# First prompt tile and sample tile taken through the stages side by side, in an encoder-trunk kernel on eight cores

## The reference

```python
h = _rmsnorm(x, norm_g); proj = h @ w_in                      # 1024 -> 4608
a, g_a, u, v, g_b, r_a, r_b = split(proj)
pa  = (trailing-window mean of a, windows 2/4/8/16 per group) - a
y_a = (silu(g_a) * (pa @ w_pool * pool_scale)) @ w_a
y_b = (silu(g_b) * u * (W_s layernorm(v) + b)) @ w_b          # chunks of 128 (64 for samples)
x + (sigmoid(r_a) * y_a + sigmoid(r_b) * y_b) @ w_o, then a final rmsnorm
```

## Time and profile before

| | |
|---|---|
| time, median of 3 runs | 867.98 us (865.93 to 882.57) |
| time of the profiled execution | 866.63 us, slowest core's span 865.2 us, others from 858.9 us |
| TensorE busy | 806.2 us, 93% of the span |
| DVE, ACT, POOL busy | 484.1, 279.5, 143.8 us |
| mean granted TensorE clock, slowest core | 0.972 |
| TensorE in 40 slices of 21.6 us, tenths | `4397998899999999999969999999999999999996` |
| granted clock in the same slices | `9778999999999999999979999999999999999999` |
| the chain that ended last | PE 86%, DMA 6%, POOL 2%, DVE 2% |

### The profile page before, as it was taken

How to read it: one execution, slowest core, us unless ns; L and a number is a source line. 1 busy time by engine, 2 the same in 40 slices (tenths; PEclk the granted TensorE clock), 3 DMA queues, 4 the chain that set the end, 5 groups by cost and what they waited for, 6 DMA issues and landing times.

```text
span 865.2 us, 13033 instructions; the slowest of 8 cores (858.9 to 865.2 us)
## 1 busy us (share of the span) xinstructions
PE 806.2 (93%) x3909; PEld 386.4 (45%) x3979; DVE 484.1 (56%) x739; ACT 279.5 (32%) x463; POOL 143.8 (17%) x353
## 2 busy tenths in 40 slices
PE   4397998899999999999969999999999999999996
PEld 2143443344444444444448644444444444444442
DVE  2334544666557655754457575557564665567445
ACT  3232233324233323332325333324232424242322
POOL 2351003111031102200142220022011201031001
PEclk9778999999999999999979999999999999999999
DMA  8599705551314040305051240315013411320202
GB/s 183 98 143 164 175 1 133 111 195 26 122 61 136 12 135 25 125 5 134 21 208 34 74 147 1 101 46 195 1 41 107 148 48 30 117 90 8 100 1 98
DMA packets 52483, 77.84 MB, mean 90 GB/s; under 512 B 34872, under 2 KB 35012, under 8 KB 52160
## 3 DMA queue, kind: packets, MB, share of 16 engines
q1 hardware_dynamic: 47568, 62.83, 22.2%
q0 software_dynamic: 4848, 14.19, 10.1%
HBM read 64.43 MB, written 18.50 MB: 96 GB/s over the span
## 4 chain that ended last, share of the span: by engine, by line
PE 86%; DMA 6%; POOL 2%; DVE 2%; issue 2%; ACT 1%; SPq 1%; POOLq 0%; DVEq 0%; ACTq 0%
PE ps L330 70%; PE ps L498 14%; DMA xr<-xh 3%; DMA Wo<-w_o 2%; PE ps L455 1%; DVE tmp L413 1%; DMA hT<-xn 1%; PE ps L273 1%; SPq L239 1%; DVE xn L297 0%; POOL Win L239 0%; POOL tmp L368 0%; POOL tmp L366 0%; ACT junk L289 0%; DVE pa L420 0%
## 5 line engine op out<-in xcount | busy, mean ns | idle before, releaser
L330 PE MATMUL ps<-hT,Win 128*128 128x512 bf16 (+1 forms) x2258 | 491.3, 369 | 2.6 <-issue 0.2
L330 PEld LDWEIGHTS ps<-hT,Win 128*128 128x128 bf16 x2304 | 225.7, 99 | 240.2 <-issue 2.4
L485 DVE TENSOR_TENSOR tmp<-ps,tmp 128x512 f32<-128x512 f32 (+1 forms) x72 | 47.6, 662 | 145.4 <-PE ps L330 141.9
L280 POOL TENSOR_SCALAR stats<-stats 128x1 f32<-128x1 f32 (+1 forms) x103 | 20.5, 199 | 616.3 <-ACT junk L289 291.4
L498 PE MATMUL ps<-Wo,mg 128*128 128x512 bf16 x531 | 119.2, 383 | 2.8 <-DMA Wo<-w_o 2.1
L479 ACT ACTIVATE tmp<-ps 128x512 f32<-128x512 f32 (+1 forms) x72 | 41.3, 574 | 141.0 <-PE ps L330 140.9
L498 PEld LDWEIGHTS ps<-Wo,mg 128*128 128x128 bf16 x544 | 53.5, 99 | 67.7 <-issue 4.8
L413 DVE TENSOR_TENSOR tmp<-tmp 128x512 f32<-128x512 f32 (+7 forms) x90 | 60.2, 669 | 37.2 <-ACT tmp L399 24.4
L510 DVE TENSOR_TENSOR xr<-ps,xr 128x512 f32<-128x512 f32 x68 | 46.9, 689 | 50.9 <-PE ps L498 50.8
L330 PE MATMUL ps<-s_bf,Wb 128*128 128x512 bf16 (+1 forms) x284 | 69.8, 367 | 0.2
L330 PE MATMUL ps<-fa,Wa 128*128 128x512 bf16 (+1 forms) x281 | 69.5, 367 | 0.4
(11 more groups left out here) (85 smaller groups left out, 482.8 us busy)
## 6 DMA issues: line engine op xcount, KB each, us to landing
xr<-xp SPq DMA_DIRECT2D x64, 512.0 KB, 6.8
yp<-xr SPq DMA_DIRECT2D x32, 512.0 KB, 2.6
Win<-w_in POOLq DMA_DIRECT2D x18, 512.0 KB, 16.4
Wo<-w_o POOLq DMA_DIRECT2D x2, 1024.0 KB, 17.7
xr<-xs SPq DMA_DIRECT2D x4, 512.0 KB, 4.6
Wa<-w_a POOLq DMA_DIRECT2D x4, 256.0 KB, 20.3
Wb<-w_b POOLq DMA_DIRECT2D x4, 256.0 KB, 21.3
ys<-xr SPq DMA_DIRECT2D x2, 512.0 KB, 4.4
```

The lines of the kernel that those rows point to most:

```text
L330: ins = e.matmul(out=bank[:, 0:cols_n], lhsT=l, rhs=r, start=(i == 0), stop=(i == n - 1))
L485: S.add("dve", lambda e: e.tensor_tensor(out=sa[:, 0:T], in0=ya[:, 0:T], in1=sa[:, 0:T], op=ALU.mult), [kya, ksa], [ksa])
```

## The change

The sample tile becomes the second tile. Tile 0 and the sample tile are prepared together (six subs, all transposed by TensorE), and then pass A, B, M and O side by side; only from the third tile on does each tile go alone. So that both fit, the sample tile's hT, `fa` and `s_bf` share one hT buffer, its normalised v goes to `junk` and its merged rows to `n_buf`. The small copies between `sl` and `carry` or `tails` move from POOL to DVE (the one into `sl` now after the ACT copy, the one back at the group's end). Only two blocks of w_in are loaded ahead of the preparation; the other loads stand between the POOL operations of the six subs, and the last 18 behind them in one row. b_s and final_g are spread at the start, copied by DVE. The halo's products are split per group (`carry_in`). The mixing matrices are loaded by SP.

```diff
-    tiles.insert(min(SAMPLE_AT, NT - 1), Tile(True, 0, False, False))
+    tiles.insert(1, Tile(True, 0, False, False))
...
+            if t.sample:
+                assert b == 1
+                t.hT = v_(hTf[1][:, 0:8 * TS], 8)
+                t.fa = v_(hTf[1][:, 8 * TS:12 * TS], 4)
+                t.s = v_(hTf[1][:, 12 * TS:16 * TS], 4)
+                t.n = v_(junk[:, :], 2)
+                t.mg = v_(n_buf[:, :], 8)
+                t.khT = [("hT", 1, s) for s in range(t.ns)]
+                t.kfa = [("fas", g) for g in range(4)]
+                t.ks = [("ss", g) for g in range(4)]
+                t.kn = ["junk"] * 2
+                t.kmg = [("n", j // 2) for j in range(8)]
...
-        def a_group(t, b, g):
+        def a_group(t, g):
             sl, ksl = next_tmp()
             L = 80 if t.sample else H + TP
+            bank, bk = win_group(t, C_A + g * P)
             if t.sample:
-                S.add("pool", lambda e: e.tensor_copy(out=tv(sl, 0, H, True), in_=tails[:, g, :].rearrange(
-                    "p (s h) -> p s h", s=4)), [("tails", g)], [ksl])
-            else:
-                S.add("pool", lambda e: e.tensor_copy(out=sl[:, 0:H], in_=carry[:, g, :]), [("carry", g)],
-                      [ksl])
-            bank, bk = win_group(t, b, C_A + g * P)
-            if t.sample:
+                tg = tails[:, g, :].rearrange("p (s h) -> p s h", s=4)
                 S.add("act", lambda e: e.activation(out=tv(sl, H, L, True), in_=bank[:, 0:TS].rearrange(
                     "p (s l) -> p s l", s=4), func=AF.Copy), [bk], [ksl])
-                S.add("pool", lambda e: e.tensor_copy(out=tails[:, g, :].rearrange("p (s h) -> p s h", s=4),
-                                                      in_=tv(sl, L - H, L, True)), [ksl], [("tails", g)])
+                S.add("dve", lambda e: e.tensor_copy(out=tv(sl, 0, H, True), in_=tg), [("tails", g)], [ksl])
             else:
-                S.add("act", lambda e: e.activation(out=sl[:, H:L], in_=bank[:, :], func=AF.Copy),
-                      [bk], [ksl])
-                S.add("pool", lambda e: e.tensor_copy(out=carry[:, g, :], in_=sl[:, TP:TP + H]),
-                      [ksl], [("carry", g)])
-            bank2, bk2 = win_group(t, b, C_GA + g * P)
+                S.add("act", lambda e: e.activation(out=sl[:, H:L], in_=bank[:, :], func=AF.Copy), [bk], [ksl])
+                S.add("dve", lambda e: e.tensor_copy(out=sl[:, 0:H], in_=carry[:, g, :]), [("carry", g)], [ksl])
+            bank2, bk2 = win_group(t, C_GA + g * P)
...
+            if t.sample:
+                S.add("dve", lambda e: e.tensor_copy(out=tg, in_=tv(sl, L - H, L, True)), [ksl], [("tails", g)])
+            else:
+                S.add("dve", lambda e: e.tensor_copy(out=carry[:, g, :], in_=sl[:, TP:TP + H]), [ksl],
+                      [("carry", g)])
...
-            S.add("dve", lambda e: e.memset(Wnat_s, 0.0), [], kWns)
-            dma("pool", Wnat_p, ws_v, [], kWnp, "w")
-            dma("pool", Wnat_s[0:64, :, 0:64], ws_v[0:64, :, 0:64], kWns, ["Wns0"], "w")
-            dma("pool", Wnat_s[64:128, :, 64:128], ws_v[0:64, :, 0:64], kWns, ["Wns1"], "w")
+            dma("sp", Wnat_p, ws_v, [], kWnp, "c")
+            dma("sp", Wnat_s[0:64, :, 0:64], ws_v[0:64, :, 0:64], kWns, ["Wns0"], "c")
+            dma("sp", Wnat_s[64:128, :, 64:128], ws_v[0:64, :, 0:64], kWns, ["Wns1"], "c")
```

272 lines of the change are left out of this document (126 added, 146 removed).

## The result

The changed kernel takes 897.51 us (median of 4 runs, 896.86 to 897.86); the kernel before, beside it on the same chip, 868.45. The ratio is 1.034 with a 95% interval of 1.032 to 1.037: slower by more than the scatter, and 15.5 us above the forecast of 882. The profiled execution has 897.6 us, a span of 895.5 on its slowest core (core 7) and 889.5 to 895.5 over the cores.

What follows compares the result with a forecast made beforehand. TensorE, busy 93% of the span, was taken as the bound, its gaps and slow stretches open to change. Start 82.3, stage A 37.3 and the rest 760.9 gave 880.5 us span, plus 1.4: 882 us, range 867 to 893.

Steps and rivals of the forecast that it cites:

- The removed waits: Tile 1 and sample tile: waits for hT, w_o and `pa` with their slow stretches go, 21.5 us off.
- The three products end between 15 and 18 us; I take 16.4.: Start, sub 0: products spreading b_s and final_g precede its scaling; square of sub 1 at 20.8 us.
- the early end: Start: the three products end at 15 us if their rows pass sub 1 by three; sum 1.5 us lower.
- No weight or row load binds here.: Preparation up to stage A: loads cost nothing, with one or two w_in blocks issued per 11.7 us round.
- TensorE waits some 7.6 us: Stage A of the pair: TensorE waits for DVE's 27.3 us of work and resumes at 33.1 us.
- Stage B starts 4.25 later as before.: End of the pair's stage A: stage B starts 4.25 us after TensorE resumes, 37.3 after stage A's start.
- Stage B to the end: From stage B's start to the kernel's end: 789.3 - 21.5 - 10.8 + 3.9 = 760.9 us.
- The small copies: Stage A of later tiles: copies on DVE cost 0.4 us per tile, 2.8 over seven, bounds 0 and 1.25 per tile.
- in full: Rival, stage A of later tiles: nothing absorbs the small copies, 8.8 us instead of 2.8, 888 us; chance 0.20.
- The warm start: Rival, preparation: TensorE stays at 2.4 GHz, 12 us less, 870 us (866 to 875); chance 0.15.
- The reordering does nothing: Rival, whole kernel: gains and losses equal, 868 us, needing a start 14 us shorter than worked out; chance 0.05.
- The short start: Rival, preparation: ACT's round does not close, subs follow their loads, stage A near 50 us, kernel 850; chance 0.08.

Runs made afterwards that it cites:

- e1: Changed kernel with the square and scaling of sub i+1 issued ahead of sub i's transposes, sub i-2's normalization behind them; median span 868.0 us against 893.
- e8: Changed kernel with SP issuing the rows b_s and final_g ahead of sub 1's 512 KB; median span 888.8 us against 893.
- e3: Changed kernel with the loads of cp, w_s and the sample's ln_g and ln_b issued in the rounds of subs 2 and 3; median span 885.6 us against 893.
- e13: e11 with GpSimd's four sample row operations waiting for the sample's last s, at stage B's end; 842.4 us, 0.971 of the kernel before.
- e11: e6 with the sample's n rows in xn buffers, its row operations issued behind stage A, and the w_s buffer's memset ahead of it; median span 842.7 us.
- e15: Changed kernel with the halo's copy into the slab ahead of the group's matmuls and ACT's slab copy; 915.8 us, 1.055 of the kernel before.
- e14: e13 with the small copies of the six lone prompt tiles on GpSimd, the pair's on DVE; median span 838.0 us, the same as e13.
- e7: e6 with the 16-column copies of stage A on GpSimd; median span 855.5 us against 849.2.
- e12: Kernel before with the small copies of stage A on DVE at their old places; median span 883.3 us against 862.
- e6: Changed kernel with squares two subs ahead, spreads behind the loop, early cp, row, w_s and halo loads, invc memsets first; 851.2 and 852.9 us, 0.984 of kernel before.

## Why the prediction was wrong

**Direction and main mechanism: right.** It said slower by 14 us, through an engine order that makes one sub cost a round of 11.7 us; rounds took 10.8 to 11.5, the v products 2.9 to 3.6, stage A started 39.6 us later than before (31.8 predicted), and e1 shows that opening the round gives 25 us back. The removed waits are gone, and nothing new came in merge or output stages. Three terms of the sum were too small, and their misses of 3.9, 5.6 and 5.0 us make the error; of the prediction's own signs the start of stage A (79 to 86 us, measured 90.1) and the single wait for DVE of 7 to 8 us (measured 3.9 and 6.0) failed with them.

**"The three products end between 15 and 18 us; I take 16.4."** They ended at 20.5, outside the bounds. I bounded the landing of b_s by that of sub 1, and took for sub 1 the 12.4 us of the kernel before. In the changed kernel sub 1 lands 13.2 us after its issue at 2.71, at 15.9, and b_s was there at 15.1: the bound held, the landing time under it did not. Why sub 1 lands later was not tried. e8 puts some 4 us on the place in SP's list. The Trainium skill's rule that I set against it ("DMA: Bandwidth & Descriptors", "Queues, rings and completion order": completion is not in order of issue) is not contradicted, but b_s passed sub 1 by 0.8 us and not by three; with the early end the sum would have been 1.5 us further off.

**"No weight or row load binds here."** This was the largest failed step, 5.6 us in the way from the square of sub 5 to stage A (20.3 instead of 14.7). cp, w_s, ln_g and ln_b are issued by the changed code only when the last round is over, and I costed them at nothing; my reason spoke of the weights alone. SP issued cp from 80.68 on, and it held TensorE for 6.25 us, until 89.25. In e3 the wait is gone and stage A starts 6.7 us earlier.

**"TensorE waits some 7.6 us" in stage A, 37.3 in all.** The sum has a slip: my own prices give 14.9 and 8.4 us for the groups, not 15.1 and 8.6, and 26.9 for DVE, not 27.3, so TensorE would resume at 32.4 and not 33.1. The prices themselves were good: in e13, undisturbed, DVE's first copy starts at 55.8 and its last ends at 83.7, 27.9 us with its small waits. What failed is the assumption that DVE would run through at the durations of single rows. It began earlier than costed (3.95 us after the start of stage A, not 6.0), but from there to the memset ahead of the setup it needed 33.6 us instead of 26.1. Two waits for buffers that the sv stores held cost 2.9 us, two waits for ACT's slab copies 3.3, and two 16-column operations beside GpSimd's row operations took 1.14 and 1.15 us instead of 0.17 and 0.18. TensorE then waited 3.93 us early in the stage, and the next 16 matmuls took 6.37 us instead of 3.61; the granted clock was 0.56 from 107 to 114 us. That a wait is followed by a slow stretch stands in the earlier trace rows too, which I used for a price and not as a warning.

**"Stage B starts 4.25 later as before."** Right as a number (128.15 to 132.40). But I let TensorE resume only when DVE's whole list of stage A is done, as before. e11 shows that this follows from the place of one memset alone. The kernel before has the same memset at the same place (L588) and a 5.47 us wait for it; there it was not tried.

**Stage B to the end: 760.9 against 763.1, and 758.8 to 761.0 in the experiments but e15.** The 2 us go with the clock. In the profiled execution the granted clock from 132 to 158 us, in the first stage B, was 0.87 on core 7 and 0.97 on core 0, where stage B to the end took 760.6 us (889.5 less 128.9). It was 0.87 to 0.90 on cores 4 to 7, with 762.5 to 763.7 us to the end, and 0.93 to 0.97 on cores 0 to 3, with 760.6 to 761.8. Core 7, then core 0:

```profile
132.00:158.00 26.00, 26.00 (x159) 15.56 (x159) 12.43 (x24) 3.93 (x8) 0.00 (x0) 0.87 0.96 163
```
```profile
132.00:158.00 26.00, 25.84 (x167) 15.90 (x169) 14.73 (x28) 6.29 (x11) 0.00 (x0) 0.97 0.85 154
```

Why it fell there on one half of the cores was not tried, and stays open.

**The small copies: 2.8 us over seven tiles.** The waits for `carry` in the later tiles add up to 3.5 us in eight waits, the longest of 1.45 us in the first lone tile; by e14 and e7 the copies cost 1.2 to 1.6. The rival "in full" did not occur here, but e15 and e12 show how near a larger cost was: with the other order of two writes, 18 to 21 us. For one such copy the traces mostly say 0.16 to 0.20 us where DVE runs alone. The section "The TRN2 errata" of the Trainium skill's page "VectorE: DVE Perf Modes" has two figures: its table, which I used, gives 0.08 us for 16 columns, and the formula below it, (N + 151) cycles at 0.96 GHz, which the page states for an fp32 addition of two tensors, gives an estimate of 0.174 for 16 columns, which agrees.

**The rivals.** The warm start (870) lost: the v products behind the 7 us waits took 3.0 to 3.6 us, where two in the unbroken stretch of e1 took 1.89. "The reordering does nothing" (868) lost too. The short start (850) lost as a description of this kernel, and e6 to e14 show what was behind it: with the orders mended the same change gives 842 us (e13), faster than the kernel before by 3%.

## What to carry to other kernels

When code moves, read each engine's list for closed rounds (a wait on one engine that hangs, through the others, on a later entry of its own list) and for what stands behind a waiting instruction. Give every load in the moved part its issue time and a landing time of its own; "loads are cheap here" has to be shown for each. Two writers of one buffer on different engines form an order of their own, which can cost more than the work moved. A single small instruction at the end of a backlogged engine's list (a memset of 0.27 us) can hold another engine for 6 us.

## What the hardware showed that was not expected

- GpSimd's two-input row operations and DVE's additions excluded each other: 0.69 us became 1.50 to 1.80 (e11), and four 16-column scalings went from 1.27 us to 4.08 (e6).
- A wait inside stage A cost TensorE up to 2.8 us more than its length: behind waits of 3.05, 3.93 and 7.05 us (e6, the changed kernel, e1) the next 16 matmuls took 5.30, 6.37 and 5.91 us instead of 3.61. Behind the 1.13 us wait in e13 they took 3.61. The length of the wait does not tell the cost: behind 2.35 us in e3 (core 4) they took 3.61 too.
- A 2 KB row issued behind a 512 KB load was used 12 us after its issue, 0.8 us ahead of that load's landing (changed kernel); issued ahead of it, 8.7 us after its issue (e8). The four cache loads of 30 KB took 8.6 us from the first issue to their use.
